# Four bank pairs for the first transposes, norms ahead of low parts, raw copies behind them, and zero products in TensorE's waits

## What is computed

```python
h   = rms_norm(x, pre_mix_norm)             # x * rsqrt(mean(x*x) + eps) * w
proj = h @ w_in                             # 1024 x 1024 by 1024 x D_PROJ
fq, fk, fv, ff, gq, gk, gv, gb, ga, gz = split(proj)
fox_o = rms_norm(forgetting_attention(fq, fk, fv, log_sigmoid(ff + fox_f_bias)), fox_out_norm)
gdn_o = rms_norm(gated_delta_chunked(silu(conv(gq, gk, gv)), g(ga), sigmoid(gb)), gdn_out_norm) * silu(gz)
x = x + rms_norm(concat(fox_o, gdn_o) @ w_out, post_mix_norm)
x = x + rms_norm(square(relu(rms_norm(x, pre_mlp_norm) @ w_up)) @ w_down, post_mlp_norm)
```

## Time and profile before

| | us |
|---|---|
| median of 3 runs | 1355.09 (1353.64 to 1355.31) |
| the profiled execution, its device time | 1352.18 |
| its span, first to last instruction | 1350.3 |
| mean granted TensorE clock | 0.997 of full |
| TensorE matmul busy | 1300.7 (96%) |
| VectorE, ScalarE, GpSimd busy | 904.3, 643.3, 541.8 |

### The profile page before, as it was taken

One profiled execution on the slowest core, in us unless ns is written; L12 is line 12 of the kernel. 1 busy time (PEld: TensorE's weight loads), 2 busy tenths in 40 slices (PEclk: granted clock), 3 DMA queues, 4 the chain that ended last, 5 costly groups with the idle time before them and its releaser, 6 DMA issues. The chain is left out here.

```text
span 1350.3 us, 19878 instructions
## 1 busy us (share of the span) xinstructions
PE 1300.7 (96%) x7003; PEld 1094.9 (81%) x7003; DVE 904.3 (67%) x1499; ACT 643.3 (48%) x1377; POOL 541.8 (40%) x438
## 2 busy tenths in 40 slices
PE   5999999999899999999999899999999999999996
PEld 4778888888798989998887688888887888888885
DVE  6987766676668777855558985556555764444567
ACT  6655333434857576772336223332332444444453
POOL 3843332324524333334024775566543554441011
PEclk9999999999999999999999999999999999999999
DMA  6243233326624061233221654355337973335333
GB/s 202 63 126 93 73 116 125 125 94 215 199 64 118 19 163 48 54 89 102 94 94 47 187 180 143 124 169 171 124 127 266 346 259 94 102 94 194 125 94 148
DMA packets 144137, 178.02 MB, mean 132 GB/s; under 512 B 19820, under 2 KB 91676, under 8 KB 144040
## 3 DMA queue, kind: packets, MB, share of 16 engines
q1 hardware_dynamic: 144040, 176.76, 40.8%
HBM read 123.72 MB, written 53.00 MB: 131 GB/s over the span
## 5 line engine op out<-in xcount | busy, mean ns | idle before, releaser
L3580 PE MATMUL ps<-db_hi,da_hi 128*128 128x512 f32 x448 | 175.2, 391 | 4.2 <-DVE db_lo L2820 4.2
L3581 PE MATMUL ps<-db_lo,da_hi 128*128 128x512 f32 x448 | 174.3, 389 | 0.0
L3582 PE MATMUL ps<-db_hi,da_lo 128*128 128x512 f32 x448 | 174.3, 389 | 0.0
L2818 DVE TENSOR_TENSOR da_lo<-a_raw,da_hi 128x512 fp32r<-128x512 f32 x112 | 85.3, 761 | 121.1 <-ACT da_hi L2198 121.1
L2198 ACT ACTIVATE da_hi<-a_raw 128x512 fp32r<-128x512 f32 x112 | 70.7, 631 | 161.5 <-PE ps L3582 139.0
L3567 PE MATMUL ps<-bt_hi,ring_hi 128*128 128x512 f32 x320 | 126.5, 395 | 7.0 <-DVE ring_lo L2722 5.3
L3569 PE MATMUL ps<-bt_hi,ring_lo 128*128 128x512 f32 x320 | 125.5, 392 | 0.0
L3568 PE MATMUL ps<-bt_lo,ring_hi 128*128 128x512 f32 x320 | 124.6, 389 | 0.0
L3203 PE MATMUL ps<-i_bt_hi,i_ring_hi 128*128 128x512 f32 x280 | 111.0, 396 | 3.2 <-DVE i_ring_lo L2290 1.8
L3205 PE MATMUL ps<-i_bt_hi,i_ring_lo 128*128 128x512 f32 x280 | 110.3, 394 | 0.0
L3204 PE MATMUL ps<-i_bt_lo,i_ring_hi 128*128 128x512 f32 x280 | 109.9, 393 | 0.0
(11 more groups left out here) (400 smaller groups left out, 3371.2 us busy)
## 6 DMA issues: line engine op xcount, KB each, us to landing
a_raw<-act_dram SPq DMA_DIRECT2D x112, 256.0 KB, 2.6
act_dram<-s_act SPq DMA_DIRECT2D x64, 256.0 KB, 2.2
wd<-in_w_down_dram SPq DMA_DIRECT2D x15, 1024.0 KB, 6.5
act_dram<-c SPq DMA_DIRECT2D x48, 256.0 KB, 4.8
w_top<-in_w_up_dram SPq DMA_DIRECT2D x16, 512.0 KB, 4.3
w_bot<-in_w_up_dram SPq DMA_DIRECT2D x16, 512.0 KB, 5.5
i_top<-in_w_in_dram SPq DMA_DIRECT2D x14, 512.0 KB, 4.0
i_bot<-in_w_in_dram SPq DMA_DIRECT2D x14, 512.0 KB, 5.3
```

The costliest lines, as they stand in the source:

```text
L2818: nc.vector.tensor_tensor(da_lo[s][:, :], a_raw[n % 4][:, :], da_hi[s][:, :].bitcast(F32), ALU.subtract).then_inc(d_lo_ready, 1)
L3580: nc.tensor.matmul(acc, da_hi[s][:, cols], db_hi[s][:, :], start=start, stop=False, skip_group_check=True)
L3581: nc.tensor.matmul(acc, da_hi[s][:, cols], db_lo[s][:, :], start=False, stop=False, skip_group_check=True)
L3582: return nc.tensor.matmul(acc, da_lo[s][:, cols], db_hi[s][:, :], start=False, stop=stop, skip_group_check=True)
```

## The change

Tiles 0 to 3 are transposed into four separate bank pairs: banks 6 and 7, 2 and 3, 0 and 1, 4 and 5. TensorE no longer waits for a low part before tiles 2 and 3. From tile 4 on it waits for both readers of the pair that it takes over. Product (0,1), which writes bank 0, also waits for the raw copy of tile 2, and (1,1) for that of tile 3.

On ScalarE the raw copy of tiles 0 to 3 now waits for the low part of the tile instead of the reverse, and stands behind high parts and squares. The gate weights' rounding moves behind the square of tile 6. On VectorE the norms of tiles 2 and 3 stand ahead of the low parts of tiles 0 and 1, and the weight low parts `i_lo` of (0,1) and (1,1) change place.

On TensorE each of the first four transposes has matmuls of zeros ahead of it: 80, then 16, 16 and 12, all bf16 128x128, into banks 4 and 5. VectorE clears the zero tile with its first instruction. After product (0,1) the order is tile 4, (1,1), tile 5, (0,2), tile 6, (1,2), tile 7; before, each product had the transpose of one tile more ahead of it.

```diff
+WARM = (80, 16, 16, 12)
...
+        warm = placed("warm", 147392, [P, P], BF16)
...
         def x_banks(t):
-            return banks(6 if t % 2 == 0 else 2, 2)
+            return banks({2: 0, 3: 4}.get(t, 6 if t % 2 == 0 else 2), 2)
+        def x_banks_before(t):
+            return t - 4 if t < 6 else t - 2
...
         @block.scalar
+            def x_square_of(t):
+                act.wait_ge(group_loaded[t], 16)
+                if t >= 1:
+                    act.wait_ge(x_square, t)
+                nc.scalar.activation(x_sq[:, :], x_in[t % 6][:, :], ACT.Square, accum_out=x_ss[:, t:t + 1]).then_inc(x_square, 1)
+            def x_high(t):
+                act.wait_ge(x_turned, t + 1)
+                nc.scalar.activation(i_ba_hi[:, :, t * P:(t + 1) * P], x_banks(t).rearrange("p (k m) -> p k m", k=KT), ACT.Copy).then_inc(x_hi, 1)
+            def x_copy(t):
                 act.wait_ge(x_turned, t + 1)
                 turned = x_banks(t).rearrange("p (k m) -> p k m", k=KT)
                 if t < HT:
+                    act.wait_ge(x_lo, t + 1)
+                    nc.scalar.activation(i_raw[:, :, t * P:(t + 1) * P], turned, ACT.Copy).then_inc(x_raw, 1)
                 else:
+                    nc.scalar.activation(i_b22[:, :, (t - HT) * P:(t - HT + 1) * P], turned[:, HK:KT, :], ACT.Copy).then_inc(x_raw, 1)
...
+            x_square_of(0)
+            x_square_of(1)
+            x_square_of(2)
+            x_high(0)
+            x_square_of(3)
+            x_high(1)
+            i_hi(0, 1)
+            x_copy(0)
+            x_high(2)
+            x_square_of(4)
+            x_high(3)
+            for t in range(1, HT):
+                x_copy(t)
+            i_hi(1, 1)
+            x_square_of(5)
+            p1_out(0)
+            i_hi(0, 2)
+            x_copy(4)
+            x_square_of(6)
+            act.wait_ge(gate_w_loaded, 48)
+            nc.scalar.activation(gate_w_hi[:, :, :], gate_w[:, :, :], ACT.Copy).then_inc(gate_w_hi_ready, 1)
+            x_square_of(7)
+            x_copy(5)
             i_hi(1, 2)
             p1_out(1)
+            x_copy(6)
             bt_hi_part(5, 0)
             bt_hi_part(3, 0)
-            x_out(NT - 1)
+            x_copy(NT - 1)
...
         @block.vector
                     dve.wait_ge(x_hi, t + 1)
-                    dve.wait_ge(x_raw, t + 1)
                     nc.vector.tensor_tensor(i_ba_lo[:, :, cols], turned, i_ba_hi[:, :, cols].bitcast(F32), ALU.subtract).then_inc(x_lo, 1)
                 else:
                     dve.wait_ge(x_turned, t + 1)
+                    dve.wait_ge(x_raw, t - HT + 1)
...
+            nc.vector.memset(warm[:, :], 0.0).then_inc(warm_ready, 1)
+            x_mean_of(0)
+            x_norm(0)
+            x_mean_of(1)
+            x_norm(1)
+            x_mean_of(2)
+            x_norm(2)
+            x_mean_of(3)
+            x_out(0)
+            x_norm(3)
+            x_out(1)
+            i_lo(0, 1)
+            x_out(2)
+            x_mean_of(4)
+            x_out(3)
+            x_norm(4)
+            i_lo(1, 1)
+            x_mean_of(5)
+            x_norm(5)
+            x_out(4)
+            i_lo(0, 2)
+            x_mean_of(6)
+            x_norm(6)
+            x_mean_of(7)
+            x_out(5)
+            x_norm(7)
             x_out(NT - 2)
             i_lo(1, 2)
...
         @block.tensor
             def turn_x(t):
                 pe.wait_ge(x_normed, t + 1)
-                if t >= 2:
-                    pe.wait_ge(x_lo, t - 1)
+                if t >= HT:
+                    pe.wait_ge(x_lo, x_banks_before(t) + 1)
+                    pe.wait_ge(x_raw, x_banks_before(t) + 1)
...
                 elif (f, i) == (0, 1):
                     pe.wait_ge(x_lo, HT)
+                    pe.wait_ge(x_raw, HT - 1)
+                elif (f, i) == (1, 1):
+                    pe.wait_ge(x_raw, HT)
...
+            def warm_up(count):
+                for _ in range(count):
+                    nc.tensor.matmul(x_banks(3)[:, 0:P], warm[:, :], warm[:, :], start=True, stop=True)
+            pe.wait_ge(warm_ready, 1)
+            warm_up(WARM[0])
             pe.wait_ge(ident_loaded, 16)
-            for t in range(5):
+            for t in range(HT):
                 turn_x(t)
+                if t < HT - 1:
+                    warm_up(WARM[t + 1])
             in_up(0, 1)
+            turn_x(4)
+            in_up(1, 1)
             turn_x(5)
-            in_up(1, 1)
+            in_up(0, 2)
             turn_x(6)
-            in_up(0, 2)
+            in_up(1, 2)
             turn_x(7)
-            in_up(1, 2)
```

More of the change, by code:

```diff
@@ L1004, in build @@
         fox_exp = sem("fox_exp")
+        warm_ready = sem("warm_ready")
         fox_turned = sem("fox_turned")
@@ L1683, in _ @@
         def _(act):
-            def x_out(t):
+            def x_square_of(t):
[7 more added lines that the diff above has]
+            def x_copy(t):
                 act.wait_ge(x_turned, t + 1)
@@ L1687, in x_out @@
                 if t < HT:
-                    cols = slice(t * P, (t + 1) * P)
-                    nc.scalar.activation(i_ba_hi[:, :, cols], turned, ACT.Copy).then_inc(x_hi, 1)
-                    nc.scalar.activation(i_raw[:, :, cols], turned, ACT.Copy).then_inc(x_raw, 1)
-                else:
-                    cols = slice((t - HT) * P, (t - HT + 1) * P)
-                    nc.scalar.activation(i_b22[:, :, cols], turned[:, HK:KT, :], ACT.Copy).then_inc(x_raw, 1)
+                    act.wait_ge(x_lo, t + 1)
+                    nc.scalar.activation(i_raw[:, :, t * P:(t + 1) * P], turned, ACT.Copy).then_inc(x_raw, 1)
+                else:
+                    nc.scalar.activation(i_b22[:, :, (t - HT) * P:(t - HT + 1) * P], turned[:, HK:KT, :], ACT.Copy).then_inc(x_raw, 1)
             def i_hi(f, i):
@@ L1778, in post @@
                     nc.scalar.activation(tile, tile, ACT.Copy, scale=FOX_DIM ** -0.5).then_inc(post_done, 1)
-            for t in range(NT):
-                act.wait_ge(group_loaded[t], 16)
-                if t >= 1:
-                    act.wait_ge(x_square, t)
-                nc.scalar.activation(x_sq[:, :], x_in[t % 6][:, :], ACT.Square, accum_out=x_ss[:, t:t + 1]).then_inc(x_square, 1)
-                if t == 3:
-                    i_hi(0, 1)
-                if t == 4:
-                    i_hi(1, 1)
-                if t == 5:
-                    act.wait_ge(gate_w_loaded, 48)
-                    nc.scalar.activation(gate_w_hi[:, :, :], gate_w[:, :, :], ACT.Copy).then_inc(gate_w_hi_ready, 1)
-                if t >= 2:
-                    x_out(t - 2)
-                if t == 6:
-                    i_hi(0, 2)
-                    p1_out(0)
-            x_out(NT - 2)
+            x_square_of(0)
[21 more added lines that the diff above has]
+            x_copy(5)
             i_hi(1, 2)
             p1_out(1)
+            x_copy(6)
             bt_hi_part(5, 0)
             bt_hi_part(3, 0)
-            x_out(NT - 1)
+            x_copy(NT - 1)
             bt_hi_part(5, 1)
@@ L2297, in bt_lo_part, with x_mean_of, x_norm @@
                 nc.vector.tensor_tensor(i_bt_lo[i][:, :, cols], i_bt_raw[i][:, :, cols], i_bt_hi[i][:, :, cols].bitcast(F32), ALU.subtract).then_inc(x_bt_lo, 1)
-            for t in range(NT):
+            def x_mean_of(t):
                 dve.wait_ge(x_square, t + 1)
                 nc.vector.tensor_scalar(x_ms[:, t:t + 1], x_ss[:, t:t + 1], 1.0 / D, EPS, ALU.mult, ALU.add).then_inc(x_mean, 1)
-                if t >= 2:
-                    x_out(t - 2)
+            def x_norm(t):
                 if t == 0:
@@ L2310, in _ @@
                                                op0=ALU.mult, op1=ALU.mult).then_inc(x_normed, 1)
-                if t == 4:
-                    i_lo(0, 1)
-                if t == 5:
-                    i_lo(1, 1)
-                if t == 6:
-                    i_lo(0, 2)
+            nc.vector.memset(warm[:, :], 0.0).then_inc(warm_ready, 1)
[24 more added lines that the diff above has]
+            x_norm(7)
             x_out(NT - 2)
```

## The result

The median of the changed kernel is 1357.36 us (1355.66 to 1361.51, 9 runs), beside 1353.53 us for the kernel before on the same chip (1352.17 to 1355.31, 9 runs): a ratio of 1.0025, 95% interval 1.0016 to 1.0034. That is 0.25% or 3.8 us slower. A second set of 12 runs of the same kernel gave 1357.2 us and a ratio of 1.0019 [1.0003, 1.0035]. The forecast was 1355.4 in a range that holds the result, but its likeliest case was no change that can be told, and the result lies just outside that. The profiled execution of the changed kernel took 1356.11 us, its span is 1354.2, where before it was 1350.3.

A forecast was written before the change was run, and what follows sets the result against it. TensorE was 96% busy, with the start of (0,6) set by a full serial chain of VectorE and GpSimd. Terms of -0.6 if the clock holds and about +1.2 if not gave +0.3: 1355.4 us, range 1351.8 to 1358.4.

The forecast's parts named there:

- likeliest case: Whole kernel: no change that can be told, about 0.2% (2.7 us) being what a measurement can tell; chance 0.68.
- what counts: Head: the change is worth what it moves the start of product (0,6), then 56.16; everything later is untouched.
- what eats the lead: 27 to 54 us: VectorE and GpSimd fill the stretch, so (0,1) starting 4.5 us earlier gives (0,6) only 0.5.
- the shared operands: 27 to 54 us: VectorE and GpSimd operations reading SBUF hold each other off, e.g. 0.68 becoming 1.77 us.
- the sum: Start of (0,6): -0.6 us if the clock holds, about +1.2 if it falls in the first gap; taken as +0.3.
- One serial chain: 27 to 54 us: VectorE and GpSimd operations laid end to end make 27.7 us in a stretch of 27.1.
- what is late next: After (0,1): power 6 ends at 27.3, so GpSimd's first long operation starts at 27.3, against 27.19 before.
- the term for the clock: Idle gaps before (0,1) and (1,2): one stretch at half clock costs about 1.7 us, delaying the chain by up to 1.8.
- rival 2: Between 20 and 56 us: the clock falls twice or more, TensorE becomes the bound; +2.8 us, 1357.9 us; chance 0.15.
- The rule against the change: Head: the skill says full clock doesn't come on for transposes, so 12 or 16 small products between might not hold it.
- Rival 3: Head: zero products don't raise the pace; (0,1) at about 22 at half pace, (0,6) at 57.5, 1356.4 us; chance 0.15.

The follow-up runs named there:

- experiment 6: Changed kernel, 56 zero products ahead of (0,1), squares and means moved forward, weight low part of (1,2) ahead of norm 7: 1355.18 us, 1.0006.
- experiment 7: Changed kernel with squares, means and weight parts of (1,2) forward, zero products ahead of (0,1), the gates and (0,6): 1355.86 us, 1.0015.
- experiment 12: Changed kernel with the head reordered to be shorter, its gaps filled with zero products and the later waits with spare products: 1354.01 us, 1.0002.
- Experiment 2: Changed kernel with 56 zero products ahead of (0,1) and 80 between tile 6 and (1,2), filling both gaps: 1354.1 us, 0.9997.
- experiment 8: Kernel before with GpSimd's eight differences cut to 8 tokens, so the output is incomplete: 1350.84 us, 0.9962.
- Experiment 1: Changed kernel with 56 zero products in TensorE's first gap, ahead of (0,1): 1356.42 us, 1.0016.
- experiment 11: Changed kernel with zero products in both gaps of the head and spare products in TensorE's longest later waits: 1353.20 us, 0.9993.
- experiment 4: Kernel before, order untouched, with zero products ahead of and between its first five transposes and ahead of (0,1): 1358.34 us, 1.0031.
- Experiment 3: Changed kernel without any zero products and without clearing the zero tile: 1356.67 us, 1.0013.
- experiment 9: Kernel before with spare products filling TensorE's longest later waits, from 323 to 487 us and at 741.7 and 747.1: 1353.01 us, 0.9999.
- experiment 10: Changed kernel, head untouched, with spare products filling TensorE's longest later waits: 1355.08 us, 1.0003.

## Why the prediction was right or wrong

**Right for the head: what counts, and what eats the lead.** Up to 325 us the change is worth what it moves (0,6); the offset of 2.05 us stands unchanged until there. For the whole time this does not hold: experiments 6, 7 and 12 start (0,6) 1.2 to 1.4 us before 56.16 and none is faster than the kernel before. (0,1) starts at 20.89 (forecast 20.3), tile 4's transpose left the critical place, the gap before (1,2) is 4.8 us (4.6), and the lead of 3.9 us is absorbed in a stretch that VectorE and GpSimd fill together and that has kept its length, 26.7 against 27.1 us. Experiment 2 shows it without the clock: first product 3.8 us earlier, (0,6) 0.5 later.

**Right in kind, too large in use: the shared operands.** The durations of experiment 8 (1.28, 0.69, 1.75 beside an idle GpSimd, 2.23, 1.79, 2.85 beside a busy one) bear out that an operation is stretched by the other engine's work. They agree with the exclusive lock that the Trainium skill states in "SBUF — State Buffer", section "SBUF: two separate sides". But taking out eight operations, 10.2 us by the sum's own 1.27 each, moved the end of the chain by only 2.8. With them gone, VectorE waited for other things, 2.40 us for a square among them. "One serial chain" was a fair account of its length, not of what shortening a link gives. The length itself was summed a little short: two of the four weight sums take 1.75 us at their shortest in the trace of before, not 1.27.

**Wrong: the step "what is late next".** It put power 6 at 27.3 and GpSimd's first long operation with it. It was 29.59. The 2.3 us are 0.6 from the later start of (0,1) and 2.1 from its half pace (4.9 us up to tile 4's transposes, against 2.8 in experiment 2), less 0.4 in the steps behind. Square 6 stands behind the copy of (0,1) on ScalarE. I gave that copy the time of a product at full pace and treated the clock as a separate term, which reached the chain only by (0,2) and tile 5. It is not separate: ScalarE's copy of (0,1) is what the clock delays, and the whole chain hangs on it. Experiment 1 measured it: first gap filled, first long operation at 27.59.

**Wrong: the term for the clock, in size and in number.** I had one fall in the head, somewhat likelier than not, of up to 1.8 us, and took +0.3 in all. There were two falls, the first of 6.8 us in the first profile and 3.4 in the second. The second one made the half-pace (1,2) start at 38.89, behind the 36.9 from which rival 2 decides, and TensorE had no wait left before (0,6), as that rival has it. But TensorE was not what decided: its next matmul could have started at 58.1, and (0,6) starts at 58.21, 0.05 behind the end of VectorE's low part, as far behind GpSimd's first long operation as in experiment 2, where TensorE waits. With both gaps held, (0,6) came at 56.69 and 56.30 (experiments 2 and 11); with the falls, at 57.69 to 58.40. The clock reached (0,6) through the first gap alone. So rival 2 is nearest to the result, 1357.9 against 1357.36, by luck: its bound added nothing that shows, and a good part of the loss lies behind the head.

**Missing: the falls behind the head.** The sum ended at (0,6): from there on everything was taken as untouched. The instructions are, but the granted clock is not. Filling the later waits took about 2 us off the change, and filling the second gap 2.3 us between experiments 1 and 2, with (0,6) 0.4 later. With the head's gaps filled, or the later waits, no loss against the kernel before is left that can be told (0.9997, 1.0003, and 0.9993 with both). That much is shown. How the 3.2 to 3.8 us divide is not. The first two profiles give 2.05 to the head and 1.9 to what lies behind it. But the start of (0,6) moves with the execution, 56.16 and 57.28 in two profiles of the head of before, 57.69 to 58.40 in three of the change's, so the head's part is anything from 0.4 to 2.2.

Behind the head not all of the loss is the clock's. TensorE's wait for `c_raw_q` is 2.08 us in the profile of before, 2.73 and 3.11 in the two of the change, 2.88, 4.65 and 3.30 in experiments 1, 4 and 6, but 1.38 and 1.72 in 2 and 3. What makes that load early or late relative to TensorE was not tried. What decides at which of the waits the clock falls was not found either. The wait of 2.38 us at 747.1 in the profile of before was not followed by a fall, the one of 2.37 at 751.4 in the change's was. The kernel before loses 6.7 to 7.5 us of clock on average, its last stretch included; the change with its head filled loses 5.7.

**The rule against the change.** The half pace at 24.80 behind transposes was what I had set beside the Trainium skill's "TensorE: Matmul & The Clock Gate", Part 4, by which the full clock doesn't come on for transposes. Experiment 3 disagrees: with nothing but transposes up to 17.6 us, the granted clock rose. The measurement decides. (It is a statement on a transpose mode; the kernel calls the transpose instruction on float32, and the trace does not name a mode.) Rival 3, zero products that buy nothing, was right for the time (1356.67 without them, 1357.2 and 1357.36 with) and wrong in its reason: they do raise the pace, by 4.9 us, but the pace is lost in the gap before the product that needs it.

**The base.** The forecast stood on a median of 1355.09 from three runs. The 9 beside the result, those three among them, gave 1353.53, the 35, 32 and 35 later ones 1354.3, 1354.03 and 1354.03. So the level was 0.8 to 1.6 us too high, and that luck brought the forecast nearer to the result than its mechanism was: forecast +0.3, measured +3.8 and, in the second set, +3.2 against that chip's 1354.03.

## What to carry to other kernels

A lead at the start of a chain is worth nothing while two engines further on fill a stretch between them; ask what releases the first operation of that stretch, and price everything ahead of it at the pace that TensorE will have then. Making TensorE wait less early on can make it wait longer later, and a longer wait can cost twice: itself, and the stretch at half clock behind it. Where a kernel is 96% TensorE, sum the lost clock of every run beside its time, but test it before it is called the cause: filling waits with spare products undid the loss of the change, and brought the kernel before nothing that could be told. Compare several profiles before a milestone of a head is called moved.

## What the runs showed of the hardware

- The time of an execution rose by 0.5 to 0.7 us for each us of lost clock (35, 32 and 35 runs of the kernel before, correlations 0.79, 0.80 and 0.65). Beside experiments 9 to 12, runs with a granted clock of 0.997 had a median of 1351.7, those with 0.996 had 1355.4 and those with 0.993 had 1354.4, so it orders the runs only roughly. Taking 3.6 us of lost clock out of the kernel before changed its time by nothing that can be told (experiment 9).
- Transposes alone brought the granted clock to full (experiment 3). The waits of 3.06 and 3.62 us before (0,1) were each followed by 0.50. So were one of 2.43 in experiment 4 and one of 2.14 in experiment 9 before (0,6), where the 1.85 before had not been. The length of a wait alone does not tell: 2.38 at 747.1 in the kernel before was not followed by 0.50, 2.37 at 751.4 in the change was.
- Tile 4's load landed at 15.86 in the profile of before and at 16.83 in that of experiment 4, and the head followed it.
- In the kernel before the full clock came at 28.7, 30.0 and 30.7 us in three profiles (before, experiments 8 and 9). In the last, (0,6) was at 57.28 against 56.16. A difference of 1 us between two profiles of a head is not yet a finding.
- Zero products in a head that gained nothing from them came with a time 0.31% longer (experiment 4); its cause was not isolated.
